# A chunked scan on one core: the fifth doubling level's products replaced by four transposes from PSUM, in a new order

## The reference, cut to what matters

```python
def wkv_scan(state, r, w, k, v, a, b, reverse):
    def step(s, inp):
        r_t, w_t, k_t, v_t, a_t, b_t = inp
        sa = jnp.einsum('bhij,bhj->bhi', s, a_t)
        s = s * w_t[:, :, None, :] + sa[..., None] * b_t[:, :, None, :] + v_t[..., None] * k_t[:, :, None, :]
        return s, jnp.einsum('bhij,bhj->bhi', s, r_t)
    ...
    state, y = lax.scan(step, state, ..., reverse=reverse)
```

## Time and profile before

| | us |
|---|---|
| median of three runs | 2080.68 |
| lowest, highest | 2075.94, 2083.98 |
| profiled execution, its own time | 2089.22 |
| span of its instructions | 2087.4 |
| PE busy in the span | 1896.9 (91%) |
| DVE busy | 1145.5 (55%) |
| ACT busy | 772.4 (37%) |
| POOL busy | 586.7 (28%) |

### The profile page before, as it was taken

How to read it: one execution, slowest core, us unless ns; L and a number is a source line. 1 busy time by engine, 2 the same in 40 slices (tenths; PEclk the granted TensorE clock), 3 DMA queues, 4 the chain that set the end, 5 groups by cost and what they waited for, 6 DMA issues and landing times. The chain is left out here.

```text
span 2087.4 us, 57632 instructions
## 1 busy us (share of the span) xinstructions
PE 1896.9 (91%) x24716; PEld 1179.8 (57%) x24716; DVE 1145.5 (55%) x2139; ACT 772.4 (37%) x2059; POOL 586.7 (28%) x733
## 2 busy tenths in 40 slices
PE   6999999899999999999989688888888888888698
PEld 3555655445544445454434377677777777777343
DVE  4534333214675577004252377777777777777674
ACT  3211111124325652221001255555555555555332
POOL 0112111013203431001112254545545554554011
PEclk9999999999999999999999899999999999999899
DMA  8300100740014775644642333453333334333742
GB/s 342 120 21 21 41 20 0 285 148 31 30 33 131 190 204 162 197 151 154 220 148 94 100 87 96 129 140 102 102 88 106 102 94 111 90 103 78 236 151 92
DMA packets 269791, 247.77 MB, mean 119 GB/s; under 512 B 92769, under 2 KB 226145, under 8 KB 266082
## 3 DMA queue, kind: packets, MB, share of 16 engines
q1 hardware_dynamic: 269538, 244.09, 38.4%
HBM read 164.32 MB, written 79.69 MB: 117 GB/s over the span
## 5 line engine op out<-in xcount | busy, mean ns | idle before, releaser
L1019 PE MATMUL ps<-xt,w_slab 128*128 128x512 f32 (+1 forms) x800 | 297.5, 526 | 0.0
L1019 PEld LDWEIGHTS ps<-xt,w_slab 128*128 128x128 f32 x800 | 148.3, 190 | 146.3 <-issue 122.6
L1914 POOL TENSOR_TENSOR bk<-feat,growth 128x256 f32<-128x256 f32 x160 | 113.2, 729 | 239.2 <-ACT growth L1967 239.2
L2238 PE MATMUL ps<-XU,TT_second 64*64 64x128 f32 (+1 forms) x3840 | 154.4, 263 | 19.2 <-DVE TT_second L2113 8.6
L2073 DVE COPY_PREDICATED W<-mask,ps 128x128 f32<-128x128 int32 x400 | 127.2, 318 | 52.6 <-PE ps L2238 29.7
L2201 PE MATMUL ps<-ar,bk 64*64 64x192 f32 (+1 forms) x1280 | 131.8, 320 | 18.6 <-POOL ar L1930 13.5
L2204 PE MATMUL ps<-ar,bk 64*64 64x192 f32 (+1 forms) x1280 | 138.6, 329 | 6.2 <-issue 5.9
L645 PE MATMUL ps<-h,fgo 128*128 128x512 f32 x320 | 141.5, 597 | 2.4 <-PEq L202 2.4
L2238 PEld LDWEIGHTS ps<-XU,TT_second 64*64 64x64 f32 x3840 | 107.8, 133 | 35.2 <-DVE TT_second L2113 14.7
L1560 PE MATMUL ps<-w_last,gated 128*128 128x512 f32 x256 | 115.0, 609 | 2.1 <-DVE gated L1651 2.1
L2113 DVE STREAM_TRANSPOSE TT_second<-W 128x256 f32<-128x256 f32 x240 | 106.9, 445 | 8.2
(11 more groups left out here) (306 smaller groups left out, 4343.6 us busy)
## 6 DMA issues: line engine op xcount, KB each, us to landing
feat<-feature_scratch SPq DMA_DIRECT2D x160, 256.0 KB
feature_scratch<-k_feats SPq DMA_DIRECT2D x64, 320.0 KB, 5.2
feature_scratch<-k_feats SPq DMA_DIRECT2D x24, 640.0 KB, 6.7
k_feats<-in_modw SPq DMA_DIRECT2D x8, 1536.0 KB, 7.3
w_slab<-in_rwin SPq DMA_DIRECT2D x24, 512.0 KB, 6.8
V<-v_token_scratch SPq DMA_DIRECT2D x320, 32.0 KB, 2.6
fgo<-in_modw SPq DMA_DIRECT2D x8, 1024.0 KB, 8.2
fw_slab<-in_fwin SPq DMA_DIRECT2D x16, 512.0 KB, 4.5
```

What stands on the lines that cost most here:

```text
L1019: mm = pe.matmul(ps[:, bank, 0:n], (w1t if i is None else w[:, i % 2])[:, k, :], src[:, k, a:a + n], start=k == 0, stop=k == KT - 1)
L1914: g.tensor_tensor(d4(bk[s][:, :, slot, :]), fe(every, lo, 768), d4(E3[s][:]), ALU.mult).then_inc(op_ready, 1)
L2238: mm = pe.matmul(of_pos(4, b)[to, x, b, :], TT_second[at_, b, :], XU[s][at_, x, b, :], start=True, stop=True)
```

## The change

It changes the scan alone. Level 16 carries X and U: `l` always moves both, and `second_x8` copies both. Level 32 no longer makes its U by products: `second_m16` and PE's `t32` go, and `second_t32` becomes four transposes of DVE (for each head, for each of the two directions), each of 32 partitions by 2 x 32 columns, which read U's off-diagonal blocks from PSUM and write them turned into W32. `second_x16` waits for these transposes, and `mt32` for it. `mt32` writes other column positions of its bank. The order of the calls in the `period` functions of ACT, DVE and PE is new. The tile M16 goes.

```diff
-PB = {"l4": 1, "l8": 2, "l16": 3, "t32": 4, "mt32": 5}
+PB = {"l4": 1, "l8": 2, "l16": 3, "mt32": 4}
-DA = {"x0": 1, "mt1": 2, "m1": 3, "x1": 4, "w2": 5, "tt2": 6}
-DB = {"w4": 1, "tt4": 2, "w8": 3, "tt8": 4, "w16": 5, "tt16": 6, "m16": 7, "t32": 8}
+DA = {"x0": 1, "mt1": 2, "m1": 3, "w2": 4, "tt2": 5, "x1": 6}
+DB = {"w4": 1, "tt4": 2, "w8": 3, "tt8": 4, "w16": 5, "tt16": 6, "t32": 10}
...
             def second_x8(j, cc):
                 act.wait_ge(db, count("dve_second", j, cc, DB["w16"]))
-                act.activation(by_pair(XU[par(cc)])[:, 0], pair(4)[:, 0], ACT.Copy).then_inc(ab, 1)
+                act.activation(by_pair(XU[par(cc)]), pair(4), ACT.Copy).then_inc(ab, 1)
             def second_x16(j, cc):
-                act.wait_ge(pb, count("second", j, cc, PB["l16"]))
+                act.wait_ge(db, count("dve_second", j, cc, DB["t32"]))
...
@@ period of ACT @@
                     first_at(j, c + 2, 0)
+                    first_n(j, c + 2, 0)
                 if Q_:
                     r(j, c, 0)
-                if A_:
-                    first_n(j, c + 2, 0)
                 if ahead or c + 3 < NCH:
                     exps(j, c + 3)
-                if Q_:
-                    sa(j, c, 0)
                 if B_:
                     second_xu(j, c + 1, 4)
                 if A_:
                     first_at(j, c + 2, 1)
+                if Q_:
+                    sa(j, c, 0)
                 if B_:
                     second_x8(j, c + 1)
+                if A_:
+                    first_n(j, c + 2, 1)
                 if Q_ and is_lat(c):
                     y(j, c, 0)
                 if Q_:
                     r(j, c, 1)
+                if A_:
+                    first_u1(j, c + 2)
+                if Q_:
+                    sa(j, c, 1)
                 if B_:
                     second_x16(j, c + 1)
-                if A_:
-                    first_n(j, c + 2, 1)
-                if Q_:
-                    sa(j, c, 1)
-                if A_:
-                    first_u1(j, c + 2)
...
-            def second_m16(j, cc):
-                v.wait_ge(ab, count("act_second", j, cc, AB["l16"]))
-                v.transpose(flat(M16[:]), xcols(par(cc))[:, 0:256]).then_inc(db, 1)
-
             def second_t32(j, cc):
-                v.wait_ge(pb, count("second", j, cc, PB["t32"]))
-                masked(32, 4).then_inc(db, 1)
+                v.wait_ge(pb, count("second", j, cc, PB["l16"]))
+                for h in two:
+                    for k, from_, to in ((0, 32, 0), (1, 0, 32)):
+                        u = of_pos(4, 2 * k)[h * HD + from_:h * HD + from_ + 32, 1, 2 * k:2 * k + 2, to:to + 32]
+                        v.transpose(W[32][h * HD + to:h * HD + to + 32, 2 * k:2 * k + 2, from_:from_ + 32], u).then_inc(db, 1)
...
@@ period of DVE @@
                     first_mt1(j, c + 2)
+                    first_m1(j, c + 2)
+                if B_:
+                    second_w(j, c + 1, 16)
                 if Q_:
                     state(j, c, 0)
                 if B_:
-                    second_w(j, c + 1, 16)
                     second_tt(j, c + 1, 16)
-                if A_:
-                    first_m1(j, c + 2)
-                    first_x(j, c + 2, 1)
-                if B_:
-                    second_m16(j, c + 1)
                 if A_:
                     first_w2(j, c + 2)
                     first_tt2(j, c + 2)
                 if B_:
                     second_t32(j, c + 1)
+                if A_:
+                    first_x(j, c + 2, 1)
                 if Q_:
                     state(j, c, 1)
...
-                x = slice(0, 2 if k < 16 else 1)
...
-                            mm = pe.matmul(of_pos(4, b)[to, x, b, :], TT_second[at_, b, :], XU[s][at_, x, b, :], start=True, stop=True)
+                            mm = pe.matmul(of_pos(4, b)[to, :, b, :], TT_second[at_, b, :], XU[s][at_, :, b, :], start=True, stop=True)
...
-            def t32(j, cc):
+            def mt32(j, cc):
                 s = par(cc)
-                pe.wait_ge(db, count("dve_second", j, cc, DB["m16"]))
+                pe.wait_ge(db, count("dve_second", j, cc, DB["t32"]))
+                pe.wait_ge(ab, count("act_second", j, cc, AB["l16"]))
                 for b in range(B4):
                     for h in two:
                         o = own(h)
-                        mm = pe.matmul(lev(4)[o, 1, b, :], AT[s][o, pos(b), :], M16[o, pos(b), :], start=True, stop=True)
...
-                        mm = pe.matmul(lev(4)[o, 0, pos(b), :], W[32][o, b, :], XU[s][o, 0, pos(b), :], start=True, stop=True)
+                        mm = pe.matmul(lev(4)[o, 0, b, :], W[32][o, b, :], XU[s][o, 0, b, :], start=True, stop=True)
                 mm.then_inc(pb, 1)
...
@@ period of PE @@
                     l(j, b, 4)
-                if Q_:
-                    sa(j, c, 0)
                 if A_:
                     products(j, a, 1)
                 if Q_:
-                    b_state(j, c, 0)
+                    sa(j, c, 0)
                 if B_:
                     l(j, b, 8)
+                if Q_:
+                    b_state(j, c, 0)
+                if A_:
+                    u1(j, a)
                 if Q_:
                     a_state(j, c, 1)
                 if B_:
                     l(j, b, 16)
-                if A_:
-                    u1(j, a)
                 if Q_:
                     sa(j, c, 1)
-                if B_:
-                    t32(j, b)
+                if A_:
+                    l2(j, a)
                 if Q_:
                     b_state(j, c, 1)
-                if A_:
-                    l2(j, a)
                 if B_:
                     mt32(j, b)
```

More of the change, by code:

```diff
@@ L1681 @@
 PA = {"g0": 1, "g1": 2, "u1": 3, "l2": 4}
-PB = {"l4": 1, "l8": 2, "l16": 3, "t32": 4, "mt32": 5}
+PB = {"l4": 1, "l8": 2, "l16": 3, "mt32": 4}
 AA = {"at0": 1, "n0": 2, "at1": 3, "n1": 4, "u1": 5}
 AB = {"l2": 1, "l4": 2, "l8": 3, "l16": 4, "xt": 5}
-DA = {"x0": 1, "mt1": 2, "m1": 3, "x1": 4, "w2": 5, "tt2": 6}
-DB = {"w4": 1, "tt4": 2, "w8": 3, "tt8": 4, "w16": 5, "tt16": 6, "m16": 7, "t32": 8}
+DA = {"x0": 1, "mt1": 2, "m1": 3, "w2": 4, "tt2": 5, "x1": 6}
+DB = {"w4": 1, "tt4": 2, "w8": 3, "tt8": 4, "w16": 5, "tt16": 6, "t32": 10}
 LAT_ONLY = lambda n: [0, 0] + [n] * (NCH - 2)
 PER = {"first": [len(PA)] * NCH, "second": [len(PB)] * NCH, "act_first": [AA["u1"]] * NCH, "act_second": [len(AB)] * NCH,
-       "dve_first": [len(DA)] * NCH, "dve_second": [len(DB)] * NCH, "two": [2] * NCH,
+       "dve_first": [len(DA)] * NCH, "dve_second": [DB["t32"]] * NCH, "two": [2] * NCH,
        "operands": [4, 4] + [5] * (NCH - 2), "rmask": LAT_ONLY(1), "y": LAT_ONLY(2),
@@ L1733, in scan @@
     XU = [sb(f"XU{s}", [P, 2, B4, CK]) for s in two]
-    M1, M16, TT_first, TT_second = (sb(n, [P, B4, CK]) for n in ("M1", "M16", "TT_first", "TT_second"))
+    M1, TT_first, TT_second = (sb(n, [P, B4, CK]) for n in ("M1", "TT_first", "TT_second"))
     W_cols = {k: sb(f"W{k}", [P, B4 * CK + 2 * k]) for k in LEVELS}
@@ L2071, in masked @@
                 lo = 256 + LEVELS.index(k) * 128
-                u = changed(psf[:, bank * 512 + 256:bank * 512 + 512 + 2 * k], k) if k == 32 else pair_changed(bank, 256, k)
-                return v.copy_predicated(changed(W_cols[k], k), runs(mask[:, lo:lo + 128], k), u)
+                return v.copy_predicated(changed(W_cols[k], k), runs(mask[:, lo:lo + 128], k), pair_changed(bank, 256, k))
             def cums(j, cc):
@@ L2237, in l @@
                             at_, to = (own(h), row(h, crossed)) if k == 8 else (row(h, crossed), own(h))
-                            mm = pe.matmul(of_pos(4, b)[to, x, b, :], TT_second[at_, b, :], XU[s][at_, x, b, :], start=True, stop=True)
-                mm.then_inc(pb, 1)
-            def t32(j, cc):
-                s = par(cc)
-                pe.wait_ge(db, count("dve_second", j, cc, DB["m16"]))
-                for b in range(B4):
-                    for h in two:
-                        o = own(h)
-                        mm = pe.matmul(lev(4)[o, 1, b, :], AT[s][o, pos(b), :], M16[o, pos(b), :], start=True, stop=True)
+                            mm = pe.matmul(of_pos(4, b)[to, :, b, :], TT_second[at_, b, :], XU[s][at_, :, b, :], start=True, stop=True)
                 mm.then_inc(pb, 1)
```

## The result

The kernel after the change takes 2067.06 us (median of five runs, 2060.57 to 2068.44) beside 2080.68 before (2075.94 to 2085.62): a ratio of 0.9932 with a 95% interval of 0.991 to 0.9953, so 14 us faster, half of the 28 that were forecast. The profiled execution, at 2066.75 us, has the scan near the 2.4 GHz level as before. From the first last-level product to the last, as in the earlier trace rows, the scan takes 702 us, 22 less; of these 22 some 9 are the two profiled executions, since that of before lay 9 us over its median. PE is 15 us less busy, DVE 10 and ACT 14 us more.

A forecast was written before the change was run, and what follows sets the result against it. The bound was a loop through PE, ACT and DVE, 8.55 or 8.23 us a period. Head 5.75, tail 1.20 and transposes 1.12 gave 8.07, saving 28 us over 80 periods: 2052 us, range 2024 to 2088.

The forecast's parts named there:

- The turns: DVE's four new 32 x 64 transposes from PSUM: 249 ns each without overlap, 1.12 us for the block.
- Rival (a): The four DVE transposes overlap, so the period falls to 7.75 us: 54 us gained, 2027 us; chance 0.25.
- Rival (b): DVE's transposes from PSUM are dear and all on the loop: slower, 2115 us at the far bound; chance 0.14.
- The tail: From level 16 to mt32: 1.20 us plus the transposes' 1.12, in place of the old 2.85.
- The head, up to level 16: From mt32 through ACT, DVE and PE to level 16's start: 5.75 us, 0.05 later than the old 5.70.
- the condition: If DVE's x0 ends later than about 2.2 us, AT's copy, forecast at 3.16, is later by as much.
- The second term: DVE's first_XU, made from AT in the head, was taken to cost 0.94 us.
- The 50 us "taken as unchanged": Irregular stops of PE and late loads, 50 us of the scan's 724 beyond undisturbed periods, assumed to stay.
- Rival (c): SP's DMA queue takes over, or PE's stops grow by half: only 3 us gained, 2078 us; chance 0.14.

The follow-up runs named there:

- eight turns: The changed kernel with its four transposes made twice, the second four waiting for the first: 2109.99 us, ratio 1.015.
- the kernel with the late y and w4 first: The changed kernel with the second y copy behind the next period's X and U copy, and w4, tt4 before the second state addition: 2080.77 us.
- `x1` shortened: The changed kernel with x1 masking one column block in place of two or three from the second head pair on: 2066.88 us, ratio 0.9917.
- the kernel without the sixteen products: The changed kernel with y stores on GpSimd, without the sixteen products of V with XG that add to state and y: 2022.65 us.
- two turns: The changed kernel with only the first direction's two of the four transposes: 2064.69 us, ratio 0.9924.
- the shorter `x0`: The changed kernel with x0 masking one column block in place of two or three from the second head pair on: 2060.27 us, ratio 0.9895.
- Narrow products: The changed kernel with y stores on GpSimd, the sixteen products of V with XG given 16 moving columns in place of 64: 2062.79 us.

## Why the prediction was half right

**The turns.** Right. The groups of DVE by shape show them at 246 ns, where 249 was taken, and the block at 1.08 against 1.12:

```profile
L2118 DVE STREAM_TRANSPOSE W<-ps 32x64 f32<-32x64 f32 x320 | 78.7, 246 | 20.5 <-PE ps L2233 10.0
```

Starts are 0.27 to 0.29 apart in all four, so no two overlap. Rival (a) falls. By the rule of the Trainium skill that the prediction weighed (VectorE: DVE Perf Modes, the section on two Vector instructions with no wait between them) they could not overlap; the trace agrees. Rival (b) falls as well, though eight turns show that its mechanism was the right one to fear: the turns are on the loop.

**The tail.** Right but for 0.10: 2.42 against 2.32, with the wait for the X copy in place of that for M.

**The head, up to level 16.** This is the step that failed: 5.75 was forecast, 6.07 measured. With the 0.10 of the tail the latent loop came to 8.49 in place of 8.07, so 0.06 shorter than the old 8.55 and not 0.48. Over 48 latent periods that takes 20 of the 28 us away. The 32 periods with a context chunk, for which 8.07 was forecast too, have a median of 8.26 in the 9 that are undisturbed, from 7.77 to 8.98, where before has 8.23; these are too few to say more. The prediction named the condition: if `x0` ends later than 2.2, AT is later by as much. It ended at 2.34, and level 4, held by the y copy ahead of the copy of the off-diagonal result, started 0.17 after its old place; so AT came 0.26 late, and M1, `u1` and level 16 with it. The second term is first_XU. I took its 0.94 from the earlier trace rows as its price, but the trace of before already shows that it is in part a wait: in 18 of the 27 undisturbed latent periods first_XU ends at 4.74 to 4.76, though it starts anywhere from 3.80 to 4.23. In the period behind that of the earlier trace rows, also 8.55 us long, it starts at 4.18 (`mt32` at 1614.41) and takes 0.58:

```profile
1618.59 0.58 DVE L2085 COPY_PREDICATED first_XU<-mask,AT 128x256 f32<-128x256 int32 x1 [1.13 <-ACT AT L1971]
```

In after it is 0.45 in some periods and about 0.9 in others, by what GpSimd is doing. GpSimd's time line in the latent period above:

```profile
1514.97 1.42 POOL L1914 TENSOR_TENSOR bk<-feat,growth 128x256 f32<-128x256 f32 x2 [1.83 <-ACT growth L1967]
```

In a period of the kernel with the late y and w4 first:

```profile
1655.30 1.68 POOL L1914 TENSOR_TENSOR bk<-feat,growth 128x256 f32<-128x256 f32 x2 [2.08 <-ACT growth L1967]
```

In the second, first_XU takes 0.45 and GpSimd's pair is 0.26 longer. DVE's time line there:

```profile
1655.96 0.45 DVE L2088 COPY_PREDICATED first_XU<-mask,AT 128x256 f32<-128x256 int32 x1 [0.50 <-ACT AT L1971]
```

Either the one or the other is held. The Trainium skill (SBUF — State Buffer, section "Who interferes with whom") has a Vector instruction with two SBUF inputs contend with a GpSimd instruction that reads SBUF, since its second input comes through a read interface that the two share under an exclusive lock; both rows agree. So a step of the head that comes a little earlier can end at the same time: with `x1` shortened, with half of the V loads and with the stores on GpSimd AT comes 0.06 to 0.08 earlier than in after and level 16 0.01 to 0.03 (medians of 15 to 22 undisturbed latent periods).

What the head is worth without the hold is seen in the kernel without the sixteen products. Two of its periods, which start with `mt32` at 1669.85 and 1678.34 and last 8.49 and 7.80 us:

```profile
1671.65 0.53 DVE L2100 TENSOR_TENSOR XG<-ps,scan_tab 128x384 f32<-128x384 f32 x1
1673.58 0.90 DVE L2091 COPY_PREDICATED first_XU<-mask,AT 128x256 f32<-128x256 int32 x1 [0.52 <-ACT AT L1979]
...
1679.79 0.53 DVE L2100 TENSOR_TENSOR XG<-ps,scan_tab 128x384 f32<-128x384 f32 x1
1681.78 0.45 DVE L2091 COPY_PREDICATED first_XU<-mask,AT 128x256 f32<-128x256 int32 x1 [0.35 <-ACT AT L1979]
```

In the first `x0` ends at 2.33 and first_XU is held; in the second `x0` ends at 1.98, AT's copy starts at 3.14, as was forecast, and first_XU is free. Of the 28 undisturbed latent periods there 17 are of the second kind, with first_XU at 0.45 (7.79 to 8.23 us), and 10 of the first (8.41 to 8.55); one takes 10.72. Their median of 8.08 is the 8.07 of the forecast by chance: few periods are that long.

**The 50 us "taken as unchanged".** This failed too, both ways, and in the two traces most of the gain came from it, not from the loop. PE's stops are the same in sum (42 us before, 40 after, counted behind the packets as above), but a stop costs less. Latent periods with a stop and without a wait for features, in three pairs of traces (the stops as the idle over 0.25 us put down to no wait; what they cost is counted from the same trace's undisturbed median):

| | periods | mean, us | stop in each, us | cost of 1 us of stop, us |
|---|---|---|---|---|
| before; after | 16; 19 | 10.08; 9.05 | 1.19; 0.82 | 1.28; 0.68 |
| half of V: before; after | 13; 23 | 10.02; 8.93 | 1.06; 0.67 | 1.38; 0.70 |
| stores on GpSimd: before; after | 20; 33 | 10.03; 9.18 | 1.23; 0.88 | 1.19; 0.81 |

In the first pair the 48 latent periods take 446.7 and 429.0 us. Of these 17.7 us the stops account for 14 and the shorter loop for 3. Why a stop costs less is not shown. That half of the forecast was reached is thus in part luck.

The late loads went the other way. Rival (c) had their mechanism, and I gave it 0.14 because SP's waits for y came to 1.5 us a period. That was a mean. In before, SP's time line between 1208 and 1900 us already has eight stretches of more than 17 us, two periods, with no gap over 0.3 us, 203 us together; in after it has fifteen, 437 us together; with the stores on GpSimd none is longer than 9. The shorter loop did not use up a slack of 1.5 us everywhere, it ran dry in many places. I should have read SP's time line, not the sum of its waits. The size, from pairs of kernels that differ by the change alone: as it stands 14 us; with half of the V loads left out on both sides 0.9867 against 0.9973, 22 us; with the stores on GpSimd 0.9892 against 1.0015, 26 us; with the stores there and fewer products 0.9732 against 0.9812, 17 us. Each of these is good to some 5 to 8 us. So SP's queue takes part of the change's worth, 8 to 12 us in two pairs, 3 in the third; how much is not settled. Nor do the 22 and 26 bear out the forecast of 28: in those two pairs the undisturbed latent loop is 8.46 and 8.47 against 8.56, 0.1 shorter and not 0.48. Only in the fourth, where most periods are free of the hold, it is 0.4 shorter (8.22 against 8.60 in the mean).

**What stands in the way of more.** The hold of first_XU, and PE's stops. In after, all 44 idle times of PE over 0.25 us that the trace puts down to no wait (1220 to 1880 us) end 1.2 to 1.7 us behind the landing of a 16 KB packet of the instruction queue, though such moments are only 11% of the time; and between two packets' starts PE starts 253 products and weight loads (median). That PE waits there for its own instructions is the plain reading; what happens inside the queue is not shown. The Trainium skill (Advanced Engine Details and Errata, section "ISA Cache") gives lines of 16 KB or 256 instructions, and two of them; the trace agrees with the size. What makes the stops long or short is not shown. The extremes look as if a denser loop had more of them (the old order with the new products 4.3 us, eight turns 22.5, after 39.9, two turns 45.9), but the kernels between do not follow: the shorter `x0` has 30.3 and the shorter `x1` 25.5, both with shorter periods than after, and the old products in the new order 33.6 with longer ones. Narrow products changed neither number nor time and had 53.9 for 44.5, so the sum from a single trace is good to some 10 us. Why fewer products took 33 to 37 us when the stops fell by 25 is open in part: the undisturbed latent periods also fell, from 8.42 to 8.22 us in the mean, which is 10 us over 48.

## What to carry to other kernels

Judge a queue's slack by its time line in a stretch where it does not wait, not by the mean of its waits: an issuing engine that goes 8.5 us without a gap in a period of 8.5 us is a bound, whatever its idle share is. Before a loop is shortened, look for what keeps its own pace: a queue of DMA issues, an engine's instruction stream. Then test by relieving that thing on both sides of the change; the change's worth is the difference of the pairs, here 14 us as it stands and 17 to 26 relieved, each with its error. And look whether the part that was forecast moved: here the total went the right way while the undisturbed loop hardly did. A duration read from a trace can be a wait: before it is carried into a sum, compare it with the same instruction in other periods.

## What was unexpected of the hardware

- PE has idle times up to 2.4 us (before and after) in which it waits for no semaphore and which follow a packet of its own instructions by some 1.4 us; they add up to about 40 us here. Leaving out an eighth of PE's instructions, with the time of their bursts nearly kept, took 33 to 37 us.
- Transposes of 32 partitions x 64 elements from PSUM take 246 ns and start 0.27 to 0.29 apart when they lie in different quarters of the partitions. Those of 128 x 256 from SBUF take 440 to 446 ns in the same trace.
- An issue of a 32 KB DMA takes 0.62 to 0.7 us of its queue on GpSimd and on SP alike; twelve issues fill SP for a whole period.
- A masked copy of DVE with two inputs in SBUF, 128 x 256, takes 0.45 us when it is not held, 0.89 beside GpSimd's operand instructions in the period of after shown above, and 2.58 where four of them follow one another.
